# One change to the scan stage of a hybrid SSD, attention and expert block on one Trainium2 core: per-unit coefficients, first rows loaded ahead of the bulk, argument products in four row strips, and a skip product divided between GpSimd and ScalarE

## The reference, cut to what matters

```python
a_cum = jnp.cumsum(da, axis=2)
seg = a_cum[:, :, :, None] - a_cum[:, :, None, :]
decay = jnp.exp(jnp.where(lower, seg, -jnp.inf))
lmat = jnp.einsum("bcign,bcjgn->bcijg", cm, bm)[..., None] * decay
y_diag = jnp.einsum("bcijgr,bcjgrp->bcigrp", lmat, xdt)
...
y_off = jnp.einsum("bcign,bcigr,bcgrpn->bcigrp", cm, jnp.exp(a_cum), s_prev)
...
y = y + d_skip.astype(jnp.float32)[:, None] * xs.astype(jnp.float32)
y = y.reshape(b, L, D_INNER) * jax.nn.silu(z.astype(jnp.float32))
```

## Time and profile before

| | us |
|---|---|
| median of 3 runs | 2603.93 |
| lowest, highest | 2603.7, 2607.3 |
| profiled execution | 2605.13 |
| span of its trace | 2603.4 |
| scan stage in the trace | from about 1030 to about 1228 |
| one chunk of four units in its middle | 20.53 |

### The profile page before, as it was taken

How to read it: one execution, slowest core, us unless ns; L and a number is a source line. 1 busy time by engine, 2 the same in 40 slices (tenths; PEclk the granted TensorE clock), 3 DMA queues, 4 the chain that set the end, 5 groups by cost and what they waited for, 6 DMA issues and landing times. The chain is left out here.

```text
span 2603.4 us, 34473 instructions
## 1 busy us (share of the span) xinstructions
PE 2381.5 (91%) x13468; PEld 1964.2 (75%) x13468; DVE 1695.9 (65%) x1900; ACT 1139.1 (44%) x1538; POOL 492.3 (19%) x425
## 2 busy tenths in 40 slices
PE   7899999999999997898999799997963999999992
PEld 2788888887798877565777599997753788888882
DVE  5555555535315762676777667655556899999996
ACT  3333333221123111354677644433332777777772
POOL 0000000222002440597010000002323011101112
PEclk9899999999999999799999899998876999999996
DMA  6222234877525784998221498894326899999994
GB/s 227 61 83 75 78 107 113 190 215 261 174 99 186 271 300 150 299 295 282 77 88 42 127 265 254 237 268 142 125 102 272 310 402 406 404 398 396 396 363 145
DMA packets 325417, 565.21 MB, mean 217 GB/s; under 512 B 21813, under 2 KB 232773, under 8 KB 301401
## 3 DMA queue, kind: packets, MB, share of 16 engines
q1 hardware_dynamic: 298890, 459.00, 51.4%
q0 software_dynamic: 23856, 99.20, 12.6%
q10 hardware_dynamic: 2528, 5.06, 0.6%
HBM read 451.69 MB, written 106.26 MB: 214 GB/s over the span
## 5 line engine op out<-in xcount | busy, mean ns | idle before, releaser
L2629 DVE TENSOR_TENSOR e_wlo<-e_w,e_whi 128x2048 fp32r<-128x2048 f32 x188 | 425.6, 2290 | 41.9 <-ACT e_whi L2578 40.5
L2578 ACT CAST e_whi<-e_w 128x2048 fp32r<-128x2048 f32 x192 | 365.4, 1909 | 123.5 <-PE e_gu L2755 82.3
L452 PE MATMUL f_lat<-h_hi,w_hi 128*128 128x512 f32 x800 | 253.8, 398 | 9.0 <-DVE w_lo L603 9.0
L452 PE MATMUL f_lat<-h_lo,w_hi 128*128 128x512 f32 x800 | 251.3, 395 | 0.0
L452 PE MATMUL f_lat<-h_hi,w_lo 128*128 128x512 f32 x800 | 251.2, 395 | 0.0
L2089 PE MATMUL b_acc<-b_hi,b_whi 128*128 128x256 f32 x768 | 218.8, 285 | 7.9 <-issue 7.9
L2089 PE MATMUL b_acc<-b_lo,b_whi 128*128 128x256 f32 x768 | 218.1, 284 | 0.0
L2089 PE MATMUL b_acc<-b_hi,b_wlo 128*128 128x256 f32 x768 | 218.1, 284 | 0.0
L452 PEld LDWEIGHTS f_lat<-h_hi,w_hi 128*128 128x128 f32 x800 | 137.9, 189 | 39.4 <-DVE w_lo L603 10.0
L452 PEld LDWEIGHTS f_lat<-h_hi,w_lo 128*128 128x128 f32 x800 | 140.1, 188 | 29.7
L452 PEld LDWEIGHTS f_lat<-h_lo,w_hi 128*128 128x128 f32 x800 | 140.1, 188 | 29.6
(11 more groups left out here) (368 smaller groups left out, 5406.9 us busy)
## 6 DMA issues: line engine op xcount, KB each, us to landing
e_w<-in_w_gate_up SPq DMA_DIRECT2D x128, 1024.0 KB, 11.6
e_w<-in_w_down SPq DMA_DIRECT2D x64, 1024.0 KB, 9.7
w_raw<-in_w_in SPq DMA_DIRECT2D x50, 512.0 KB, 4.1
t_space<-xbcT POOLq DMA_DIRECT2D x18, 1280.0 KB, 6.4
before<-t_space SPq DMA_DIRECT2D x16, 1024.0 KB, 4.5
shared<-before SPq DMA_DIRECT2D x64, 256.0 KB, 6.8
l_w<-in_w_ssd_br SPq DMA_DIRECT2D x20, 768.0 KB, 6.8
xbcT<-t_out POOLq DMA_DIRECT2D x20, 640.0 KB, 4.4
```

The lines of the kernel that those rows point to most:

```text
L452: mm = nc.tensor.matmul(o, weights[:, b, k, :], part[:, k, a:a + n], start=(k == 0 and n_pass == 0), stop=(k == KT - 1 and n_pass == 2))
L2578: nc.scalar.copy(whi[:, slot % SPLIT], w[:, slot]).then_inc(w_hi, 1)
L2629: V.tensor_tensor(wlo[:, slot % SPLIT], w[:, slot], whi[:, slot % SPLIT].bitcast(F32), ALU.subtract).then_inc(w_split, 1)
```

## The change

In the scan stage, and in what the stage before it stores for it:

1. The rows of sums and logarithms go to one scratch tensor `lines`, stored in pieces of 4096 bytes instead of 512.
2. The four argument products of a unit take their 18 rows from four strips of partitions, which begin at 0, 32, 64 and 96, instead of all from partition 0. `own_cum` and `all_cum` are laid out so. `all_cum` now has a buffer for a whole chunk, two of them, filled by eight DMAs of one partition each, issued together once in a chunk on ScalarE's queue. `exponents(u)` waits for both exponentials of the unit before, where it waited for them half by half.
3. The coefficients are made for each unit apart, after `weigh`: one reduction and one operation on 8 columns, in place of four reductions and two operations on 32 columns before `weigh` once in a chunk. TensorE's `between` waits for the last of them.
4. The skip product is divided: GpSimd does 256 of the 512 columns, ScalarE the other four heads as four activations (`skip_rest`), after `scale_back`.
5. At the start SyncE issues chunk 0's own rows first, then the tables, B and C, and group 0; then it waits until these own rows, the constants and the rows of both buffers of `all_cum` have landed, and only then issues the rest. z of chunk 0 comes group by group. All rows of ones are set by twelve small VectorE instructions at the start.

```diff
+        strip_lines = lines.rearrange("(d g h) k r c i -> c h d (k r) g i", d=2, g=GROUPS, h=HALVES)
+        strip_cums = lines.rearrange("(d g h) k r c i -> c h d k g r i", d=2, g=GROUPS, h=HALVES)
...
+            for a, (half, d) in enumerate(STRIPS):
+                eng.dma_start(own_cum[n % NB][STRIP * a + 2:STRIP * a + ROWS].bitcast(F32), strip_lines[n, half, d]).then_inc(cum_in[n % NB], 16)
...
+                    if n == 0:
+                        load_own(sp, 0)
                     sp.dma_start(bc[j].rearrange("p a g q -> p (a g q)"), bcF[n]).then_inc(bc_in[j], 16)
...
+                        if n == 0:
+                            sp.dma_start(z[0][:, cols], zT[0:P, cols]).then_inc(group_in[0][g], 16)
+                            if g == 0:
+                                sp.wait_ge(cum_in[0], 64)
+                                sp.wait_ge(const_in, 32)
+                                for k in range(2):
+                                    sp.wait_ge(rows_in[k], 16 * 12)
...
-                    for half in range(HALVES):
-                        if u >= 1:
-                            pe.wait_ge(exps_made, HALVES * (u - 1) + half + 1)
-                        for d in range(2):
-                            mm = nc.tensor.matmul(arg_ps[:, half, d], own_cum[j][0:ROWS, d, HALVES * g + half, :],
-                                                  all_cum[0:ROWS, u % RB, d, LANES * half:LANES * half + LANES, :], start=True, stop=True)
-                        mm.then_inc(args_made, 1)
+                        pe.wait_ge(rows_in[n % RB], 128 * (n // RB) + 192)
+                    if u >= 1:
+                        pe.wait_ge(exps_made, HALVES * u)
+                    for a, (half, d) in enumerate(STRIPS):
+                        rows = slice(STRIP * a, STRIP * a + ROWS)
+                        mm = nc.tensor.matmul(arg_ps[:, half, d], own_cum[j][rows, g, :], all_cum[rows, n % RB, g], start=True, stop=True)
+                        if d == 1:
+                            mm.then_inc(args_made, 1)
...
+                def load_rows(n):
+                    if n >= RB:
+                        act.wait_ge(args_made, HALVES * G * (n - RB + 1))
+                    for a, (half, d) in enumerate(STRIPS):
+                        for k in range(2):
+                            act.dma_start(all_cum[STRIP * a + k:STRIP * a + k + 1, n % RB].bitcast(F32), strip_cums[n, half, d, k:k + 1]).then_inc(rows_in[n % RB], 16)
...
+                def skip_rest(u):
+                    n, g, j = where(u)
+                    act.wait_ge(coef_made, u + 1)
+                    act.wait_ge(group_in[j][g], group_count(n, g))
+                    if u >= 2:
+                        act.wait_ge(diag_read, u - 1)
+                    for h in range(LANES, HPG):
+                        cols, col = slice(PDIM * h, PDIM * h + PDIM), HPG * g + h
+                        ins = nc.scalar.activation(skip[:, u % 2, cols], x[j][:, 512 * g + PDIM * h:512 * g + PDIM * h + PDIM], ACT.Copy,
+                                                   scale=coef[:, n % 2, col:col + 1])
+                    ins.then_inc(rest_made, 1)
...
+                    V.tensor_tensor_reduce(gdump[:], g_ps[:, g, :], diagonal[:], 1.0, NEG, ALU.add, ALU.max, gdiag[:, g:g + 1]).then_inc(coef_step, 1)
...
+                    V.scalar_tensor_tensor(coef[:, n % 2, h], tab[:, j, DT, 0, h], gdiag[:, g:g + 1], dskip[:, h], ALU.mult, ALU.add).then_inc(coef_made, 1)
...
                     if u + 1 < UNITS:
-                        if g == 0:
-                            coefficients(n)
                         weigh(u + 1)
+                        coefficients(u + 1)
                     add_inside(u)
...
-                    nc.gpsimd.tensor_tensor(heads(skip[:, u % 2]), heads(x[j][:, 512 * g:512 * g + 512]),
-                                            spread(coef[:, n % 2, HPG * g:HPG * g + HPG]), ALU.mult).then_inc(skip_made, 1)
+                    nc.gpsimd.tensor_tensor(heads(skip[:, u % 2, 0:256]), heads(x[j][:, 512 * g:512 * g + 256]),
+                                            coef[:, n % 2, HPG * g:HPG * g + LANES].unsqueeze(2).to_broadcast([P, LANES, PDIM]), ALU.mult).then_inc(skip_made, 1)
```

110 lines of the change are left out of this document (49 added, 61 removed).

## The result

| | before | changed |
|---|---|---|
| median of 4 runs | 2605.61 us (2603.70 to 2610.63) | 2623.55 us (2621.56 to 2626.83) |
| ratio | | 1.006, 95% interval 1.0045 to 1.0075 |
| profiled execution, span | 2603.4 us | 2619.8 us |
| first DMA issue of the scan stage | 1030.25 | 1032.09 |
| last product of unit 4 on GpSimd, from that issue | 61.4 | 67.5 |

Of the 16.4 us between the two spans 12.2 lie in the scan. The rest lies ahead of it (1.8) and behind attention's start (2.4), where all profiles of this study scatter: the scan starts between 1026 and 1039, and from attention's start to the end it is 1374.5 to 1380.0. So I compare the scan from its own first issue, and the median of a run can differ from what its one profile shows by several us.

What follows compares the result with a forecast made beforehand. TensorE, GpSimd and the DMA engines were taken as nearly full in the scan, with the store path as next bound; 9.7 (steady part) + 4.7 (start) = 14.4 saved from 2603.93 gives 2589.5 us, range 2579 to 2602.

Steps and rivals of the forecast that it cites:

- The steady part: Scan, unit 4 to 31: chunk falls from 20.53 to 19.1 us, saving 9.7 us (3.6 to 11.7).
- The start: Scan start: holding back bulk loads brings first copies near 1042 and unit 4 at 1087, saving 4.7 us (1.7 to 7.7).
- Strips, skip product, ScalarE's share: Per scan unit: four argument products 0.50 us, GpSimd's half skip product 0.60, ScalarE's four activations 0.87.
- The 0.37: Four argument products in strips: 1.13 / 3.07 = 0.37 us by the Trainium skill's speedup, for a chunk of 17.5.
- They are covered: ScalarE, each chunk: eight row DMAs at 0.27 take 2.2 us, hidden because the exponentials wait 2.3 after the coefficients anyway.
- issues above 0.6: Sign of being wrong: ScalarE's row DMAs show issues above 0.6 us.
- `between` ... up to 0.5: TensorE's `between`: adds 1.1 us and now also waits up to 0.5 for the coefficients of the unit before.
- The store path at 19.1: Scan stores on SyncE's queue: issue and landing take 22.7 us, so a chunk's period can't fall below 19.1.
- The row DMAs hold ScalarE: Rival, chance 0.07: eight issues at t cost 8t - 2.3 in six chunks; at t = 1.0 34 us, 2623.
- The DMA engines take it: Rival, chance 0.16: DMA engines limit the scan to 20.2 a chunk, 1 us at the start; 3.2 saved, 2600.7.

Runs made afterwards that it cites:

- e8: Changed kernel with a chunk's coefficients made together again, ahead of the weighing of its first unit; 2607.0 us, ratio 0.9995.
- e2: Changed kernel without SyncE's wait ahead of the bulk loads at the start; 2617.4 us, ratio 1.0025.
- e11: Changed kernel with coefficients per chunk, row DMAs in 2 KB pieces, no SyncE wait, stores of units 0 to 29 on ScalarE's queue; 2598.6 us, ratio 0.9957.
- e19: e11 with the argument products of each chunk's third unit issued four times to fill TensorE's gap; 2586.6 us, ratio 0.9912.

## Why the prediction was wrong, step by step

Forecast 2589.5 in a range of 2579 to 2602, measured 2623.55. Two terms failed. The steady part was to save 9.7 us with a chunk of 19.1; it took 22.3, and unit 4 to 30 lost 5.7. The start was to save 4.7; it lost 6.1. In the steady part the step that failed is the wait on the last unit's coefficients and what is queued behind it, in the forecast's words the cover of the row DMAs and the wait of `between`.

- **Strips, skip product, ScalarE's share:** right. 0.51 for four products (0.50 taken), 0.614 (0.60), 1.06 for four activations (0.87 taken, a fifth too little). GpSimd's unit is 4.55 to 4.57 wherever it is the bound, as reckoned. The 0.37 that the prediction worked out beside its own 0.50 was not reached.
- **"They are covered":** the step that failed for the chunks. An issue costs 0.61 and not 0.27: I took the median of a DMA of two pieces of 4 KB for one of sixteen pieces of 512 bytes. The prediction's own sign of being wrong, issues above 0.6, came up. And the cover was reckoned from the exponentials' side alone. I had put a wait on the unit's own coefficients ahead of the burst without asking what is queued behind it; the burst of 5.1 starts at 1167.31, where ScalarE's queue would have been free for it at about 1164.6, when the activations of `scale_back` start (an estimate from e8, whose burst starts with them). e8 takes the wait away and leaves the burst: 12.0 us less from unit 4 to 30.
- **"`between` ... up to 0.5":** it waits 1.3 on average and up to 2.0, since the last unit's coefficients stand behind the weighing and their small operation lasted until GpSimd's product had ended.
- **The clock** was in no term. Every relief was reckoned at 1.00, because the earlier trace rows shows 1.00. It shows that for a TensorE busy 19.71 of 20.
- **The start, -4.7:** it was +6.1. Rows were issued until 1048.6 (1040 taken), the hold ended at 1053.2 (1042 taken). What then happened was as said: store 0 stands behind everything, unit 4 waits for it to land. The place was right and the size off by 11, in the wrong direction: the hold was taken for a gain, and e2 shows it as a loss of 4.6.
- **The store path at 19.1:** right as a mechanism at the start (9.5, 12.2 and 16.2 us of waiting in three kernels, and e11 takes it away) and once the seams are shorter (1.25 and 0.94 us in e8), and not what set 22.3. That e19 has 19.16 a chunk is chance: its stores don't take that path.
- **The rivals.** "The row DMAs hold ScalarE" had 0.07 and named the main mechanism. With t = 0.61 its own formula gives 2.6 x 6 = 15.5 lost against 14.4 won, 2605. The other 18 us are 11 at the start and about 4 outside the scan, in places where executions scatter; the rest falls to the wait of `between` and the clock, which its formula leaves out and no run divides. "The DMA engines take it" (20.2 a chunk) is refuted by e19's 19.16 and e11's two chunks of 19.2: at a DMA share of 1.0 they move up to 386 GB/s, and no engine waits for a load in the steady part.

Not settled: how the 2.1 us by which a seam with row DMAs exceeds one without (8.2 against 6.05) divide into the burst and the clock; and what of e19's gain is the clock's. What keeps e19's chunk above GpSimd's 18.3 is in part GpSimd's wait for the coefficients, 0.7 us in each.

## What to carry to other kernels

Before an operation is moved behind another, list what is queued behind every wait on its result, DMA issues above all: one late coefficient held TensorE, a multiply and a burst of loads together. When the fullest engine is relieved, ask what its idle time does to its clock; here a gap of 1 us was followed by a drop that cost 1.7 in four chunks of six, and filling it with useless work shortened the scan by 6. And a relief must go to all engines that are nearly full, and to the queue in which the results leave.

## What the runs showed of the hardware that was not expected

- A small VectorE operation with its inputs in SBUF lasts until GpSimd's running product ends: 0.23 us alone, 0.95 from 1166.31, ending at 1167.26, where GpSimd's product ends at 1167.24. The reductions and the weighing, which read a PSUM bank, are not stretched. The Trainium skill ("SBUF — State Buffer", SBUF: two separate sides) says so: VectorE with two SBUF inputs, against a GpSimd operation that reads SBUF, and GpSimd lock a shared port pair for a whole instruction, and the other waits. The trace agrees with the times above.
- ScalarE's queue issues DMAs while up to eleven activations handed over before are still to run (e8, from 1136.78), but not past one that waits: in the changed kernel the issues start at 1167.31, with the activation that had waited until 1167.30.
- A DMA's issue time goes by its shape and not by its bytes or its number of pieces: 0.61 for sixteen pieces of 512 bytes to one partition, 0.43 in the median for 64 such pieces to 16 partitions (the own rows, below, on SyncE's queue), 0.23 to 0.28 for eight of 2 KB to two partitions, 0.33 for a store of 128 rows of 2 KB. Which part of the shape counts is not shown.

```profile
L1281 SPq DMA_DIRECT2D shared<-lines x32: 334/428/1557, 1032.1 to 1182.5; - x32
```

- TensorE at 0.93 busy was granted 1.2 GHz behind a gap of 1.0 us in four chunks of six (e11), and kept 2.4 GHz behind the same gap in the other two. With a gap of 0.3 and 0.96 busy it kept it in all six (e19).
